# Hybrid decoder block on one core: gather, scatter and bias of the expert loop in another form

## The reference

```python
logits = (xt @ w_router) + b_router
top_val, top_idx = lax.top_k(logits, TOP_K)          # 4 of 32 experts per token
gates = jax.nn.softmax(top_val, axis=-1)
...
def expert_block(args):
    toks, e = args
    xb = x_pad[toks]                                 # the tokens of this expert
    gu = xb @ w_gu[e] + b_gu[e]                      # 1024 -> 2048
    gate, lin = gu[:, :D_FF], gu[:, D_FF:]
    gate = jnp.minimum(gate, SWIGLU_LIMIT)
    lin = jnp.clip(lin, -SWIGLU_LIMIT, SWIGLU_LIMIT)
    act = (lin + 1.0) * gate * jax.nn.sigmoid(SWIGLU_ALPHA * gate)
    return act @ w_down[e] + b_down[e]               # 1024 -> 1024
...
y = jnp.einsum('tkd,tk->td', y_assign.reshape(T, TOP_K, D), gates)
```

## Time and profile before

| | |
|---|---|
| median of 3 runs | 1337.99 us (1337.21 to 1339.19) |
| profiled execution, span | 1339.1 us; no time outside its span is known |
| TensorE busy | 1299.5 us, 97% |
| VectorE, ScalarE, GpSimd busy | 299.8, 231.7, 111.7 us |
| HBM read | 441.27 MB, 331 GB/s over the span |
| DMA share in the loop's slices | 9 tenths |
| chain that ended last | PE 89%, DVE 6%, DMA 3%, ACT 1% |

### The profile page before, as it was taken

The page is one execution under the profiler, slowest core; times in us unless marked ns, Lnnn a source line. Parts: engine busy times, 40 slices in busy tenths (PEclk is TensorE's granted clock), DMA queues, the critical chain, the costliest instruction groups (busy, mean ns, idle before and its releaser), DMA issues.

```text
span 1339.1 us, 16541 instructions
## 1 busy us (share of the span) xinstructions
PE 1299.5 (97%) x6746; PEld 671.7 (50%) x6746; DVE 299.8 (22%) x527; ACT 231.7 (17%) x295; POOL 111.7 (8%) x42
## 2 busy tenths in 40 slices
PE   8689899999999999999999999999999999999998
PEld 6577899765444444444444444444444444444443
DVE  5398736322111111111111111111111111111111
ACT  2432533111111111111111111111111111111111
POOL 3355344100000000000000000000000000000000
PEclk8789899889999999999999999999999999999999
DMA  7633335566999999999999999999999999999990
GB/s 248 190 127 126 127 98 196 229 244 252 378 387 393 393 396 392 390 392 408 393 398 389 398 392 400 398 400 391 393 400 388 378 391 392 398 391 393 391 395 35
DMA packets 72586, 444.17 MB, mean 332 GB/s; under 512 B 4248, under 2 KB 8632, under 8 KB 56152
## 3 DMA queue, kind: packets, MB, share of 16 engines
q1 hardware_dynamic: 68400, 437.82, 81.6%
q10 hardware_dynamic: 4168, 6.09, 1.8%
HBM read 441.27 MB, written 2.62 MB: 331 GB/s over the span
## 4 chain that ended last, share of the span: by engine, by line
PE 89%; DVE 6%; DMA 3%; ACT 1%; issue 0%; POOL 0%; ACTq 0%; DVEq 0%; POOLq 0%
PE psum L716 33%; PE psum L750 17%; PE psum L688 9%; PE psum L694 9%; PE psum L725 4%; DMA rel_rows<-hg 3%; PE psum L741 2%; PE psum L660 2%; DVE slot_r L953 2%; PE psum L407 1%; PE psum L402 1%; PE psum L403 1%; PE psum L758 1%; PE psum L512 1%; PE psum L736 1%; DVE score L985 1%
## 5 line engine op out<-in xcount | busy, mean ns | idle before, releaser
L716 PE MATMUL psum<-ring,hg 128*64 128x512 f32 x2048 | 452.0, 594 | 0.2 <-ACT hg L893 0.2
L716 PEld LDWEIGHTS psum<-ring,hg 128*64 128x64 f32 x2048 | 144.0, 137 | 276.3 <-issue 274.2
L750 PE MATMUL psum<-ring,hg 128*64 128x512 f32 x1024 | 232.2, 595 | 0.0
L1210 DVE TENSOR_SCALAR hg<-psum 128x512 f32<-128x512 f32 x32 | 22.1, 692 | 526.6 <-PE psum L716 526.6
L750 PEld LDWEIGHTS psum<-ring,hg 128*64 128x64 f32 x1024 | 70.6, 137 | 133.3 <-issue 133.3
L688 PEld LDWEIGHTS psum<-idx_region,work 128*128 128x128 f32 x1056 | 122.9, 192 | 26.1 <-issue 26.0
L688 PE MATMUL psum<-idx_region,work 128*128 128x64 f32 x1056 | 128.4, 275 | 0.0
L694 PE MATMUL psum<-hg 128*128 128x512 f32 x264 | 122.1, 605 | 0.7 <-ACT hg L906 0.7
L898 ACT ACTIVATE hg<-hg 128x512 f32<-128x512 f32 x32 | 20.1, 629 | 524.1 <-DVE hg L1210 524.1
L1281 POOL TENSOR_SCALAR tiny<-tiny 128x1 f32<-128x1 f32 x4 | 1.2, 302 | 1072.5 <-ACT sig_a L909 1043.9
L1253 POOL TENSOR_TENSOR slot_r<-ring,slot_r 128x2560 fp32r<-128x2560 f32 x13 | 83.4, 6430 | 87.3 <-ACT slot_r L785 87.3
(11 more groups left out here) (232 smaller groups left out, 905.0 us busy)
## 6 DMA issues: line engine op xcount, KB each, us to landing
ring<-in_w_gu SPq DMA_DIRECT2D x128, 2048.0 KB, 12.9
ring<-in_w_down SPq DMA_DIRECT2D x64, 2048.0 KB, 9.8
ring<-in_w_in SPq DMA_DIRECT2D x11, 2048.0 KB, 8.3
ring<-in_w_out SPq DMA_DIRECT2D x2, 2048.0 KB, 13.0
ring<-in_w_up_a SPq DMA_DIRECT2D x1, 2048.0 KB, 10.3
ring<-in_w_up_b SPq DMA_DIRECT2D x1, 2048.0 KB, 7.9
rel_rows<-hg ACTq DMA_DIRECT2D x1, 1536.0 KB
ring<-in_w_in SPq DMA_DIRECT2D x1, 1184.0 KB, 9.0
```

What stands on the lines that cost most here:

```text
L716: last = mm(psum[half * 64:half * 64 + 64, b, :], xgT_sb[:, j * SLOTS:(j + 1) * SLOTS], slot_gu(c)[:, jj, c0:c0 + 512], start=(j == 0), st ...
L750: last = mm(psum[half * 64:half * 64 + 64, 2, :], actT_sb[:, a:a + SLOTS], slot4(s)[:, k, half * 512:(half + 1) * 512], start=False, stop= ...
```

## The change

Five parts, all in the expert loop or for it.

1. **Gather.** `pick` (128x64) becomes the stationary operand and `h2` streams past, 512 columns at a time: four products in two side-by-side pairs, into bank 3, as rows of tokens. VectorE copies them to SBUF (`xg_sb`), and four transposes (`gather_T`) bring them to the form that c0 to c3 need. The products stand between c1 and c2, the transposes behind those of the activation. The order of the tiles in `xgT_sb` changes with it.
2. **Combine.** The four products contract over 64 rows each: the stationary operand is rows 0 to 63 of `combT_sb` for one half of the output and rows 64 to 127 for the other. `comb`, of which the transposed form is made, holds the 64 columns twice instead of zeros, so two transposes do instead of four.
3. **Gate and up bias.** The four products contract over 32 rows each, each in its own group of 32 rows (`bias_gu` holds a 512-column piece in each group). They have moved from behind c2 ahead of the gather to behind c2 alone.
4. **Down bias.** No longer in the loop. Behind the loop the gates (256x32, four copies side by side, `gates4`) are transposed and multiplied with `bias_dn`, in four products of 32 rows each.
5. **Setup.** The biases come with eight DMAs on ScalarE's queue instead of two, and the clearing of `bias_region` and `padded` on GpSimd goes. Ahead of the loop the first gather takes the new form too (ScalarE copies it out).

```diff
@@ views @@
-        bias_gu, bias_dn = bias_region[:, 0:2048], bias_region[:, 2048:3072]
+        bias_gu, bias_dn = bias_region[:, 0:512], bias_region[:, 512:1024]
...
+        xg_sb = qk_region[:, 0:512]
         pick = idx_region[:, 0:128].rearrange("p (r s) -> p r s", r=NT)
-        padded = idx_region[:, 128:512].rearrange("p (r s) -> p r s", r=NT)
+        comb = idx_region[:, 128:384].rearrange("p (r s) -> p r s", r=NT)
+        gates4 = idx_region[:, 576:832].rearrange("p (r g e) -> p r g e", r=NT, g=4)
@@ tensor @@
-            def gather(part):
-                for j in range(4 * part, 4 * part + 4):
-                    for r in range(NT):
-                        last = mm(psum[:, 3, j * SLOTS:(j + 1) * SLOTS], h2[:, r, j, :], pick[:, r, :],
-                                  start=(r == 0), stop=(r == NT - 1))
-                return last
+            def gather():
+                for r in range(NT):
+                    for half in range(2):
+                        last = mm(psum[half * 64:half * 64 + 64, 3, :], pick[:, r, :],
+                                  h2[:, r, 4 * half:4 * half + 4, :].rearrange("p j q -> p (j q)"),
+                                  start=(r == 0), stop=(r == NT - 1), skip_group_check=True)
+                last.then_inc(xg_mm, 1)
+            def gather_T():
+                for c in range(4):
+                    last = nc.tensor.transpose(psum[:, 3, c * P:(c + 1) * P], xg_sb[:, c * P:(c + 1) * P], ident)
+                last.then_inc(gather_mm, 1)
             def combine(r, half):
-                return mm(psum[:, 4 + 2 * r + half, :], combT_sb[:, (half * NT + r) * P:(half * NT + r + 1) * P],
-                          y_sb, start=False, stop=True, skip_group_check=True)
+                rows = slice(half * SLOTS, (half + 1) * SLOTS)
+                return mm(psum[:, 4 + 2 * r + half, :], combT_sb[rows, r * P:(r + 1) * P], y_sb[rows, :],
+                          start=False, stop=True, skip_group_check=True)
...
                     last.then_inc(w_used[s], 1)
+                    if c == 1:
+                        pe.wait_ge(combT_ready, i + 1)
+                        pe.wait_ge(pick_ready, i + 2)
+                        gather()
                     if c == 2:
-                        pe.wait_ge(padded_ready, i + 1)
+                        pe.wait_ge(comb_ready, i + 1)
                         for b in range(2):
                             for half in range(2):
-                                c0 = b * FF + half * 512
-                                mm(psum[half * 64:half * 64 + 64, b, :], which_expert, bias_gu[:, c0:c0 + 512],
+                                rows = slice((2 * b + half) * NE, (2 * b + half + 1) * NE)
+                                mm(psum[half * 64:half * 64 + 64, b, :], which_expert[rows, :], bias_gu[rows, :],
                                    start=False, stop=False, skip_group_check=True)
-                        pe.wait_ge(combT_ready, i + 1)
-                        pe.wait_ge(pick_ready, i + 2)
-                        gather(0)
...
                 last.then_inc(actT_mm, 1)
-                gather(1).then_inc(gather_mm, 1)
+                pe.wait_ge(xg_rows_ready, i + 2)
+                gather_T()
                 pe.wait_ge(actT_ready, i + 1)
-                for half in range(2):
-                    mm(psum[half * 64:half * 64 + 64, 2, :], which_expert, bias_dn[:, half * 512:(half + 1) * 512],
-                       start=True, stop=False, skip_group_check=True)
...
-                        for q in range(2 * NT):
-                            a = (1 - q // NT) * SLOTS
-                            tr = nc.tensor.transpose(psum[:, 3, q * P:(q + 1) * P], padded[:, q % NT, a:a + P], ident)
+                        for r in range(NT):
+                            tr = nc.tensor.transpose(psum[:, 3, r * P:(r + 1) * P], comb[:, r, :], ident)
...
+            pe.wait_ge(gates_ready, 1)
+            for r in range(NT):
+                last = nc.tensor.transpose(psum[:, 3, r * P:(r + 1) * P], gates4[:, r].rearrange("p g e -> p (g e)"),
+                                           ident)
+            last.then_inc(gatesT_mm, 1)
             pe.wait_ge(y_ready, n_items + 1)
             for r, half in halves:
-                combine(r, half).then_inc(all_mm, 1)
+                combine(r, half)
+            pe.wait_ge(gatesT_ready, 1)
+            for r, half in halves:
+                rows = slice((2 * r + half) * NE, (2 * r + half + 1) * NE)
+                mm(psum[:, 4 + 2 * r + half, :], gatesT_sb[rows, r * P:(r + 1) * P], bias_dn[rows, :],
+                   start=False, stop=True, skip_group_check=True).then_inc(all_mm, 1)
@@ vector, loop @@
-                dve.wait_ge(gather_mm, i + 1)
+                dve.wait_ge(xg_mm, i + 1)
...
+                dve.wait_ge(xg_mm, i + 2)
+                v.tensor_copy(xg_sb, psum[:, 3, :]).then_inc(xg_rows_ready, 1)
```

More of the change, by code:

```diff
@@ L259, in build @@
         merge_mm, merge_ready, out_mm = sem("merge_mm"), sem("merge_ready"), sem("out_mm")
-        ffn_gain_in, moe_bias_zero, moe_bias_in, final_gain_in = (
-            sem(n) for n in ("ffn_gain_in", "moe_bias_zero", "moe_bias_in", "final_gain_in"))
+        ffn_gain_in, moe_bias_in, final_gain_in = (
+            sem(n) for n in ("ffn_gain_in", "moe_bias_in", "final_gain_in"))
         h2T_ready = [sem("h2T_ready0"), sem("h2T_ready1")]
@@ L265, in build @@
                              "router_exp", "sel_ready", "pos_mm"))
[L266 to L270, removed]
+        items_ready, items_mm, table_ready, n_items_ready = (
+            sem(n) for n in ("items_ready", "items_mm", "table_ready", "n_items_ready"))
+        xg_mm, xg_rows_ready, gates_ready, gatesT_mm, gatesT_ready = (
+            sem(n) for n in ("xg_mm", "xg_rows_ready", "gates_ready", "gatesT_mm", "gatesT_ready"))
+        pick_ready, comb_ready, gate_ready, act_ready = (
+            sem(n) for n in ("pick_ready", "comb_ready", "gate_ready", "act_ready"))
         sigm_ready, xg_ready, actT_ready, combT_ready, y_ready = (
@@ L715, in _ @@
                                 c0 = b * FF + half * 512
-                                last = mm(psum[half * 64:half * 64 + 64, b, :], xgT_sb[:, j * SLOTS:(j + 1) * SLOTS],
+                                last = mm(psum[half * 64:half * 64 + 64, b, :], xgT_sb[:, a:a + SLOTS],
                                           slot_gu(c)[:, jj, c0:c0 + 512], start=(j == 0), stop=(j == NJ - 1),
@@ L750, in _ @@
                             last = mm(psum[half * 64:half * 64 + 64, 2, :], actT_sb[:, a:a + SLOTS],
-                                      slot4(s)[:, k, half * 512:(half + 1) * 512], start=False, stop=(m == NJ - 1),
+                                      slot4(s)[:, k, half * 512:(half + 1) * 512], start=(m == 0), stop=(m == NJ - 1),
                                       skip_group_check=True)
@@ L854, in _ @@
             f(sig_a[:, 1024:2048], proj(9), ACT.Sigmoid).then_inc(evacuated[1], 1)
-            act.wait_ge(moe_bias_zero, 1)
-            act.dma_start(bias_gu[0:NE, :], b_gu[0]).then_inc(moe_bias_in, 16)
-            act.dma_start(bias_dn[0:NE, :], b_down[0]).then_inc(moe_bias_in, 16)
+            for g in range(4):
+                rows = slice(g * NE, (g + 1) * NE)
+                act.dma_start(bias_gu[rows, :], b_gu[0][:, g * 512:(g + 1) * 512]).then_inc(moe_bias_in, 16)
+                act.dma_start(bias_dn[rows, :], b_down[0][:, (g % 2) * 512:(g % 2 + 1) * 512]).then_inc(moe_bias_in, 16)
             take_high(12)
@@ L891, in _ @@
             last.then_inc(router_exp, 1)
+            act.wait_ge(xg_mm, 1)
+            f(xg_sb, psum[:, 3, :], ACT.Copy).then_inc(xg_rows_ready, 1)
             act.wait_ge(gather_mm, 1)
@@ L1189, in _ @@
             link(last)
-            dve.wait_ge(padded_zero, 1)
+            v.tensor_copy(gates4, bc(gates.unsqueeze(2), [P, NT, 4, NE])).then_inc(gates_ready, 1)
             n_items = dve.value_load(table[0:1, 2 * TAB:2 * TAB + 1], min_val=NE, max_val=MAX_ITEMS)
@@ L1216, in _ @@
                 v.tensor_tensor(act_sb, lin_sb, sig_sb, ALU.mult).then_inc(act_ready, 1)
+            dve.wait_ge(gatesT_mm, 1)
+            v.tensor_copy(gatesT_sb, psum[:, 3, 0:NT * P]).then_inc(gatesT_ready, 1)
             dve.wait_ge(final_gain_in, 16)
```

27 lines of the change are left out of this document (15 added, 12 removed).

## The result

The changed kernel takes 1253.87 us (median of 4 runs, 1251.32 to 1256.59), the kernel before 1338.59: a ratio of 0.937, 95% interval 0.935 to 0.939. The forecast was 1270 with a range of 1252 to 1302. The medians differ by 84.7 us. The profiled span is 1250.3 us, 88.8 less than the 1339.1 of before; the execution that was profiled took 1252.55 us, so some 2.2 us lie outside the span.

The account below looks back on a forecast made before the run. TensorE binds now; after the change its item takes 29.30 us instead of 31.94, so the DMAs' 30.3 binds. Loop start 311.6, 2.7, 31 items (939.3), last steps and tail gave span 1271, time 1270 us, range 1252 to 1302.

Parts of the forecast that it names:

- rival 3: In the loop `w_down` pieces stream at 418 GB/s, so TensorE and DMAs both take 29.4 us an item; 1256 us; chance 0.13.
- the DMAs' floor: Time the DMAs need for one loop item's `w_gu` and `w_down`: 30.3 us, bounds 29.4 to 30.7.
- The last step of the sum: From span 1271 to time 1270 us, because the span of before stood 1.1 above the median of the runs.
- The two phases: Loop items first run at TensorE's 29.3 us from the ring's stock of one item, later at the DMAs' 30.3.
- rival 5: The DMAs already bind the loop, floor 31.5 us an item; 14 us less, 1324, or no change; chance 0.07.
- That gains nothing: Narrow combine, 1.7 instead of 3.4 us: transposes still wait for the activation, so c3's end to the transposes stays 3.11.
- The bias: Gate and up bias behind c2: four 32-row products run together in 0.86 us, plus 0.15 for two changes, 1.01.
- rival 1: The four bias products run only two by two, 0.86 us more an item, TensorE 30.2; 1281 us; chance 0.17.
- rival 2: Bias: two row groups may not write one PSUM bank together; three steps, 2.57 us; 1309 us; chance 0.08.
- rival 6: Bias and combine: row groups neither run together nor change for free; TensorE 33.1 us an item; 1374 us; chance 0.05.
- rival 4: TensorE's new waits in the loop lower its clock, costing 1.7 us an item; TensorE 31.0, 1309 us; chance 0.05.
- The tail: Behind the loop, ScalarE's squares start only after the combine and first bias product: 1 us more, bounds -1 to +3.5.

Follow-up runs that it names:

- after_less_dma: Changed kernel, but from the second item on the last weight piece brings only 256 of its 1024 columns: 1226.42 us, ratio 0.916.
- the two wide variants: Changed kernel with the gate and up bias as before (128 rows): 1254.29 us; changed kernel with the combine as before (128 rows): 1255.96 us.
- combine_alone: Kernel before with only the new combine (64-row pairs, two transposes for four): 1311.11 us, ratio 0.980.
- after: The changed kernel itself, with all five parts, against the kernel before: 1253.87 us, ratio 0.937.
- after_long_runs: Changed kernel with `w_down` read 16 KB in a row per partition and `w_gu` columns and biases streamed with a stride: 1240.84 us, ratio 0.929.

## Why the prediction was right

**The number.** 1253.87 lies 16 us below the forecast, outside the 1262 to 1278 that was given 0.45, and only 2 us above the lower end of the range (1252). It lies beside rival 3's 1256, given 0.13, though that rival's account (both engines at 29.4) did not come true either: TensorE took 28.41 and the DMAs 29.82. The mechanism was right, the size was not, and that the time stayed in the range is partly luck. In spans, 1271 was forecast and 1250.3 measured, 20.7 less: 31 x 0.48 = 15 us are the DMAs' floor and 5.8 an earlier loop start, beyond the 0.6 that the sum had for the gather. Some 3 of these 5.8 are chance: the profile from which the sum started had the low clock at 291 us and was 3 us longer than the two later ones of the same kernel (1339.1 against 1336.1 and 1336.0). The other terms are small: 0.9 less for TensorE's steps in the last item, 0.4 more in the tail. The last step of the sum took 1 us off the span to get the time; the changed kernel's time is 2.2 above its span.

**The two phases: right.** TensorE was the bound, the ring's stock lets it run at its own pace, and then the DMAs bind. after_less_dma takes the second phase away, and the two wide variants show that the total no longer depends on TensorE, up to the 0.79 us an item that was tried. With the floor at 29.82, rival 5 (31.5) is out.

**The DMAs' floor: right in kind, too high in size.** The step was 30.3 us an item (bounds 29.4 to 30.7); it measured 29.82. `w_gu` was right (19.3 forecast; at 431 GB/s 19.5). `w_down` was not: I took 374 to 388 GB/s from stretches that I called queued, and in the changed kernel, with the queue never empty, it runs at 410, so 10.3 us (29.82 - 19.5) instead of 11.0. Cut finer, those stretches of the kernel before hold a dip:

```profile
717.90:725.00 7.10, 7.10 (x38) 2.64 (x38) 0.64 (x3) 2.48 (x3) 0.00 (x0) 1.00 0.81 281
725.00:728.00 3.00, 3.00 (x18) 1.00 (x16) 0.00 (x0) 0.00 (x0) 0.00 (x0) 1.00 0.97 322
...
1008.00:1012.00 4.00, 4.00 (x20) 1.29 (x18) 0.64 (x3) 1.88 (x2) 0.00 (x0) 1.00 1.03 421
1012.00:1014.00 2.00, 2.00 (x12) 0.71 (x10) 0.00 (x0) 0.00 (x0) 0.00 (x0) 1.00 0.90 285
1014.00:1017.00 3.00, 3.00 (x16) 1.00 (x14) 0.00 (x0) 0.00 (x0) 0.00 (x0) 1.00 1.02 408
```

By 725.0 some 2.0 MB have moved since 717.9 (281 GB/s over 7.1 us), nearly all of the first piece's 2.1 MB: the dip stands where the first `w_down` piece ends and the second begins. In the second item the pieces ran at 421 ahead of it and at 408 behind it. The dip costs about 0.6 us (3 us at 322, or 2 us at 285, instead of 410): in the second item that is all that 388 lies below 410, in the first about two thirds. In the changed kernel the same seam leaves no dip: no microsecond from 805 to 814 is below 401 GB/s. What differs there is how many pieces stand in the queue: a `w_down` piece lands 23.2 us after its issue (median over the run), in the kernel before 9.8. That this is the reason fits, but no run changed the queue alone. Rival 3 had the right direction, at 418.

**TensorE's item: 29.30 forecast, 28.41 measured.** c0 to c2 with gather, the bias at 1.01, c3, c4 and c5 came out to within 0.03 us together. Three small terms were too dear: the combine up to the transposes 2.91 (I had 3.11), the transposes up to c4 1.35 (1.92), the two scatter transposes 0.37 (0.50), together 0.90. The first two are one mistake. I read the 0.24 us that the profile puts down to VectorE ahead of the transposes as a wait for the activation, and 0.25 as the price of a hand-over. But every later weight load of the combine has the same 0.24 us of idle ahead of it, which these rows of the kernel before show beside the earlier trace rows:

```profile
707.62 3.70 PE L694 MATMUL psum<-hg 128*128 128x512 f32 x8
...
709.87 0.19 PEld L694 LDWEIGHTS psum<-hg 128*128 128x128 f32 x1 [0.24 <-issue]
710.30 0.19 PEld L694 LDWEIGHTS psum<-hg 128*128 128x128 f32 x1 [0.24 <-issue]
...
711.16 0.60 PE L736 MATMUL psum<-cst,hg 128*128 128x128 f32 x4
```

The combine did not end at 710.73, where the prediction had its end: the array went on with it, and the first transpose runs only at 711.16, 0.43 us behind its load. So the combine itself held the transposes back, not the activation. A real hand-over is 0.05 us (in the changed kernel the activation ends at 433.47, the load starts at 433.52). Hence the step "That gains nothing" failed: in combine_alone the narrow combine and its two transposes gain 0.78 an item, 27 us in all. In the changed kernel this is invisible in the total, and so the forecast did not suffer from it.

**The bias: right.** Four together, 1.01 us as forecast; rivals 1, 2 and 6 are out. Two row groups wrote bank 0, one in its lower and one in its upper 64 partitions, and two bank 1, and all four were done within 1.09 us; taking turns at a bank, as in rival 2, would have taken 2.57. The Trainium skill, TensorEngine Tiling (Array Packing), Gotcha 1: PSUM Pressure, states that different row tiles cannot access the same PSUM bank simultaneously. The measurement does not bear this out for groups that write different partitions of the bank. The runs do not show the case in which they write the same partitions.

**The clock: right.** It stayed at the full level (1.00) in the loop, though TensorE's weight loads had waits of up to 2.0 us and the array was busy in 507.23 of 550 us; rival 4 is out.

**The tail: right.** Forecast +1; from the result's copy on ScalarE (1329.10, 1238.91) to the end it was 10.0 and is 11.4 us.

## What to carry to other kernels

When an engine at 97% and a queue at a 0.95 share stand side by side, work out both floors before counting a saving: here 3.53 us an item were saved on TensorE, and in the long run 2.12 could be kept. A transfer rate averaged over a stretch in which the queue is nearly empty can understate what the DMAs will do when it is full: here the average was 374 to 388 GB/s, because of a dip between two pieces, and 410 once several stood in line. Cut such a stretch into microseconds before taking its mean for a floor. And a short wait that a profile puts down to one engine should be held against the usual idle ahead of the instructions before it: where they are equal, that engine may not be what held it.

## What the runs showed of the hardware

- Four products of 32 rows each, in four row groups and two column halves, ran in the time of two half-array ones: eight records in 1.09 us (the down bias of before, two half-array products, took 1.08). Two of 64 rows ran together as well, eight records in 1.99 instead of 3.70.
- The length of the run in HBM is worth 1.4% of the rate for the whole item: 422 GB/s with `w_down` in pieces of 4 KB, 428 with 16 KB.
- Streaming a moving operand in groups of 4 out of every 8 float32 values did not slow a 64x512 product: the mean record lasts 595 ns in both forms (after and after_long_runs, 600 to 1150 us). Transposes that read every fourth float32 value took 0.75 us for four instead of 0.66.
